# The last stage of a two-layer diffusion block: one token's eight expert rows added on VectorE and GpSimd, or on TensorE and VectorE

## The reference, cut to what matters

```python
def reference(...):
    ...
    for layer in range(2):
        ...                                   # attention, then the residual h_lat
        f_lat = modulate(rmsnorm(h_lat, g_ffn[layer]), sh_fl, sc_fl)
        if last:
            y = moe_ffn(f_lat, ...)           # per token: 8 routed experts, weighted, + a shared one
            h_lat = h_lat + gt_fl * y         # gate of the last layer
    return rmsnorm(h_lat, g_final)            # [1, 512, 1024], float32
```

## Time and profile before

| what | value |
|---|---|
| median of 3 runs (lowest to highest) | 2790.37 us (2789.46 to 2794.35) |
| the profiled execution's own time | 2796.55 us |
| its span, first to last instruction | 2794.8 us |
| last stage, first DMA issue to the end of the span | 2720.6 to 2794.8 us |
| busy between 2720 and 2795 | DVE 49.53, POOL 21.29, ACT 7.05, PE 0.00 us |

### The profile page before, as it was taken

The page is one execution under the profiler, slowest core; times in us unless marked ns, Lnnn a source line. Parts: engine busy times, 40 slices in busy tenths (PEclk is TensorE's granted clock), DMA queues, the critical chain, the costliest instruction groups (busy, mean ns, idle before and its releaser), DMA issues. The chain is left out here.

```text
span 2794.8 us, 34685 instructions
## 1 busy us (share of the span) xinstructions
PE 2368.1 (85%) x13774; PEld 1310.1 (47%) x13774; DVE 829.1 (30%) x1597; ACT 652.9 (23%) x1390; POOL 342.2 (12%) x282
## 2 busy tenths in 40 slices
PE   7899899897969999999991779996876988888860
PEld 3454577675534333333330678885743333333320
DVE  2232344533700000000003845555352000000007
ACT  1111333421112121121111344444210211111111
POOL 1000000021321111111110000000213111111103
PEclk9999999997989999999996889998988999999985
DMA  7465200012179999999965611100236999999956
GB/s 309 166 226 197 91 1 1 35 61 85 81 291 347 375 392 385 398 365 377 378 242 201 242 40 35 36 23 34 84 144 252 387 408 414 420 415 388 419 241 268
DMA packets 121023, 646.59 MB, mean 231 GB/s; under 512 B 19000, under 2 KB 30264, under 8 KB 60704
## 3 DMA queue, kind: packets, MB, share of 16 engines
q1 hardware_dynamic: 91456, 558.31, 50.9%
q0 software_dynamic: 28256, 83.95, 7.6%
q10 hardware_dynamic: 1152, 2.11, 0.2%
HBM read 604.38 MB, written 57.75 MB: 237 GB/s over the span
## 5 line engine op out<-in xcount | busy, mean ns | idle before, releaser
L1578 PE MATMUL F_psG<-gu_w,F_xT 128*32 128x512 f32 (+2 forms) x4448 | 708.4, 613 | 62.4 <-DMA gu_w<-in_we_up_dram 57.7
L1578 PEld LDWEIGHTS F_psG<-gu_w,F_xT 128*32 128x32 f32 (+2 forms) x4448 | 227.5, 123 | 471.9 <-issue 461.3
L1721 DVE TENSOR_TENSOR F_hh<-F_sil,F_psG 128x256 f32<-128x256 f32 x96 | 40.4, 421 | 1098.9 <-ACT F_sil L1665 1098.9
L1592 PE MATMUL F_psY<-d_w,F_hT 128*32 128x512 f32 (+2 forms) x2224 | 351.6, 599 | 3.0 <-ACT F_hT L1668 3.0
L1522 POOL DMA_INDIRECT y_d<-F_yb,sca x94 | 94.5, 1005 | 996.0 <-ACT F_yb L1671 996.0
L1665 ACT ACTIVATE F_sil<-F_psG 128x256 f32<-128x256 f32 x96 | 36.9, 384 | 671.9 <-PE F_psG L1578 671.9
L1592 PEld LDWEIGHTS F_psY<-d_w,F_hT 128*32 128x32 f32 (+2 forms) x2224 | 102.4, 120 | 180.6 <-issue 167.8
L1671 ACT ACTIVATE F_yb<-F_psY,wgt 128x1024 f32<-128x1024 f32 x96 | 107.0, 1115 | 291.7 <-PE F_psY L1592 291.7
L1571 PEld LDWEIGHTS F_psX<-cst,F_xb 128*128 128x128 f32 x768 | 95.7, 194 | 105.9 <-issue 71.4
L1571 PE MATMUL F_psX<-cst,F_xb 128*128 128x128 f32 x768 | 112.1, 290 | 32.0 <-DMA F_xb<-f_d,F_gi 27.2
L149 PE MATMUL I_psC<-I_w_hi,I_aT_hi 128*128 128x384 f32 (+1 forms) x336 | 112.6, 335 | 28.8 <-DVE I_aT_lo L2116 25.2
(11 more groups left out here) (342 smaller groups left out, 3166.0 us busy)
## 6 DMA issues: line engine op xcount, KB each, us to landing
gu_w<-in_we_gate_dram SPq DMA_DIRECT2D x130, 1024.0 KB, 6.6
gu_w<-in_we_up_dram SPq DMA_DIRECT2D x130, 1024.0 KB, 9.1
d_w<-in_we_down_dram SPq DMA_DIRECT2D x130, 1024.0 KB, 8.9
h<-in_w_ada_dram SPq DMA_DIRECT2D x40, 1024.0 KB
I_ring<-y_d SPq DMA_DIRECT2D x24, 1024.0 KB
H_y<-y_d SPq DMA_DIRECT2D x4, 4096.0 KB
I_w_raw<-in_wc_in_dram SPq DMA_DIRECT2D x32, 384.0 KB
wq<-in_w_ada_dram SPq DMA_DIRECT2D x8, 1024.0 KB, 4.6
```

The source lines that it names most:

```text
L1578: ins = nc.tensor.matmul(psG[c:c + n].rearrange("p (v f) -> p v f", v=2), xT[:, k, c:c + n], moe.gu[s][:, :, k], start=(k == 0), stop=(k = ...
L1592: ins = nc.tensor.matmul(psY[c:c + w, n], hT[:, j, k, c:c + w], moe.d[s][:, k, n * 512:(n + 1) * 512], start=(k == 0), stop=(k == KF - 1))
```

## The change

`stage_combine` is replaced by `stage_last`, which is written for this one call.

- SP loads each tile in 4 pieces of 2 rows (1 MB, 8 KB to a partition), 16 pieces in all. Each piece has a place of its own in SBUF (`rows`) and a semaphore of its own, so no load waits for anything.
- DVE takes pieces 0 and 1 of a tile: one addition of 2048 columns and one of 1024 (in place).
- PE takes pieces 2 and 3: it multiplies each of the 4 rows with the identity and accumulates them in PSUM (`psA`, two buffers of two banks). A bank holds 512 columns, so each row takes 2 products, and a tile takes 8.
- DVE then adds the PE's sum to its own, multiplies with the gate and adds to the residual, half by half: 6 instructions of 512 columns. POOL does nothing any more.
- ACT's work and the normalisation are as before. DVE waits once for both constants, ahead of its first addition.

```diff
-                            sp.dma_start(y8[:, t % 2], rows_of[t]).then_inc(s_ac[t % 2], 16)
+                        for t in range(NL):
+                            for n in range(PIECES):
+                                sp.dma_start(y[t][:, n], rows_of[t, :, 2 * n:2 * n + 2]).then_inc(s_y[PIECES * t + n], 16)
...
+                    @block.tensor
+                    def _(pe):
+                        for t in range(NL):
+                            if t >= 2:
+                                pe.wait_ge(s_acc, 2 * (t - 1))
+                            for n in range(PIECES - ON_PE, PIECES):
+                                pe.wait_ge(s_y[PIECES * t + n], 16)
+                                for b in range(2):
+                                    for k in range(2):
+                                        ins = nc.tensor.matmul(psA[:, t % 2, b], ident, y[t][:, n, k, b * 512:(b + 1) * 512],
+                                                               start=(n == PIECES - ON_PE and k == 0), stop=(n == PIECES - 1 and k == 1))
+                                    if n == PIECES - 1:
+                                        ins.then_inc(s_pe, 1)
...
-                            link(nc.vector.tensor_tensor(y[:, 0:4], y[:, 0:4], y[:, 4:8], ALU.add))
-                            link(nc.vector.tensor_tensor(y[:, 0:2], y[:, 0:2], y[:, 2:4], ALU.add))
-                            nc.vector.tensor_tensor(ac[:, t % 2], y[:, 0], y[:, 1], ALU.add).then_inc(s_sum, 1)
...
-                                nc.gpsimd.tensor_tensor(ac[:, t % 2], ac[:, t % 2], gate[:, 0 if t < NL else 1], ALU.mult).then_inc(s_g, 1)
-                                pool.wait_ge(s_g, t + 1)
-                                nc.gpsimd.tensor_tensor(h[:, t], h[:, t], ac[:, t % 2], ALU.add).then_inc(s_h, 1)
...
+                        dve.wait_ge(s_v, 32)
+                        for t in range(NL):
+                            for n in range(PIECES - ON_PE):
+                                dve.wait_ge(s_y[PIECES * t + n], 16)
+                            link(nc.vector.tensor_tensor(y[t][:, 0], y[t][:, 0], y[t][:, 1], ALU.add))
+                            link(nc.vector.tensor_tensor(y[t][:, 0, 0], y[t][:, 0, 0], y[t][:, 0, 1], ALU.add))
+                            if t >= 1:
                                 normed(t - 1)
+                            for b in range(2):
+                                c = slice(b * 512, (b + 1) * 512)
+                                dve.wait_ge(s_pe, 2 * t + b + 1)
+                                link(nc.vector.tensor_tensor(ac[:, t % 2, c], y[t][:, 0, 0, c], psA[:, t % 2, b], ALU.add))
+                                link(nc.vector.tensor_tensor(ac[:, t % 2, c], ac[:, t % 2, c], gate[:, c], ALU.mult))
+                                ins = nc.vector.tensor_tensor(h[:, t, c], h[:, t, c], ac[:, t % 2, c], ALU.add)
+                                ins.then_inc(s_acc, 1)
+                            dve.wait_ge(s_acc, 2 * t + 2)
+                            dve.sem_inc(s_h, 1)
+                        normed(NL - 1)
```

More of the change, by code:

```diff
@@ L1736, in _, with stage_last @@
                                 rows(s_xv)
-        def stage_combine(l, nt, aT):
+        def stage_last():
+            PIECES, ON_PE = TOPK // 2, 2
             with ExitStack() as ctx:
[L1743 to L1746, removed]
+                S = lambda n: sem(f"H_{n}_s")
+                T = lambda n, shape, dt=F32: sb(ctx, f"H_{n}", shape, dt)
+                rows = T("rows", [P, NL, PIECES, 2, D])
+                y = [rows[:, t] for t in range(NL)]
                 ac = T("ac", [P, 2, D])
-                gate = T("gate", [P, nv, D])
-                amul = T("amul", [P, nv, D])
-                aadd = T("aadd", [P, nv, D])
+                gate = T("gate", [P, D])
+                gain = T("gain", [P, D])
                 an = T("an", [P, 2, D])
[L1752 to L1759, removed]
+                st = T("st", [P, NL, 3])
+                junk = ps(ctx, "H_junk", [P, D])
+                psA = ps(ctx, "H_psA", [P, 2, 2, 512])
+                s_y = [S(f"y{g}") for g in range(PIECES * NL)]
+                s_v, s_pe, s_h, s_rt, s_out0, s_acc = S("v"), S("pe"), S("h"), S("rt"), S("o"), S("acc")
+                s_out, s_act, s_dve = [S("out0"), S("out1")], S("act"), S("dve")
+                rows_of = y_d[1].rearrange("(t p k) d -> t p k d", p=P, k=TOPK)
                 with nc.Block() as block:
@@ L1776, in _ @@
                         link = Chain(act, s_act)
[L1777 to L1793, removed]
+                        act.dma_start(gate[:], mod_rows(1, 0, 5)).then_inc(s_v, 16)
+                        act.dma_start(gain[:], a["g_final"].rearrange("(o d) -> o d", o=1).to_broadcast([P, D])).then_inc(s_v, 16)
+                        for t in range(NL):
+                            act.wait_ge(s_h, t + 1)
+                            link(nc.scalar.activation(junk[:], h[:, t], ACT.Square, accum_out=st[:, t, 0:1]))
+                            nc.scalar.activation(st[:, t, 1:2], st[:, t, 0:1], ACT.Sqrt, bias=eps, scale=1.0 / D).then_inc(s_rt, 1)
                     @block.vector
@@ L1813, in normed @@
                             if t >= 2:
[L1814 to L1823, removed]
@@ L1846, in _ @@
[L1846 to L1856 removed]
+                                dve.wait_ge(s_out[t % 2], 16 * (t // 2))
@@ L2368, in build @@
         moe_ctx.close()
-        stage_combine(1, NL, None)
+        stage_last()
         end_stage()
```

41 lines of the change are left out of this document (6 added, 35 removed).

## The result

The changed kernel takes 2777.18 us (median of 6 runs, 2774.83 to 2780.77) where the kernel before took 2793.96 in the same set of runs (2789.46 to 2796.61). The two medians differ by 16.8 us; the ratio estimated from the runs, 0.9946 with a 95% interval of 0.9935 to 0.9957, stands for some 15 us. Either way it is faster, by about half a per cent. A second set with the changed kernel and the kernel before gave 0.9954 (0.9941 to 0.9967).

The account below looks back on a forecast made before the run. The last stage was taken as bound by VectorE, stretched by GpSimd: 13.6 us a tile, falling to 9.50. Residuals end at 2772.5, plus 6.7 gives 2779.2, 15.6 earlier; 2790.4 - 15.6 = 2774.8 us, range 2770.5 to 2784.

Parts of the forecast that it names:

- the start of the loads: Last stage's loads: 1.02 MB until 2724.0, then 420 GB/s, so constants and pieces 0 and 1 landed at 2729.1.
- VectorE as the bound, and its price a tile: Last stage: VectorE's work sets the pace, 9.50 us a tile where it was 13.6.
- GpSimd as the reason for the long instructions: Last stage: GpSimd running beside VectorE added 2.1 us each to the 4096 addition and the result.
- GpSimd was not what stretched VectorE: Rival, last stage: the result stays at 3.39 us for three tiles, 6.3 us lost, 2781.1 us; chance 0.06.
- VectorE's wait for both constants costs nothing: Ahead of VectorE's first addition: constants land at the same time as the pieces it needs, so no time lost.
- The dip at tile 2: TensorE, after 3.0 us of idling ahead of tile 2: the products take 1.7 us longer.
- Slower transfers: Rival, last stage's loads: small pieces move at 360 GB/s, a gain of 11.1 us, 2779.3 us; chance 0.12.
- TensorE at the low level throughout: Rival, last stage: clock stays at 0.50, 14.06 us a tile, 2792.4 us; chance 0.09.
- The identity's load exposed at the low level: Rival, TensorE: 0.34 us identity loads stand between records, 1.22 us a record, median 2814.2 us; chance 0.04.
- The earlier clock: Rival, TensorE: clock rises early, VectorE's tile 0 wait is shorter, 1.2 us better, 2773.6 us; chance 0.07.

Follow-up runs that it names:

- e2: Kernel before with gate and residual moved from GpSimd to VectorE, loads of 4 MB kept: stage 65.8 us, median 2783.09 us, ratio 0.9972.
- e6: Changed kernel with one 4 MB load a tile, each with its own place, instead of pieces: stage 67.9 us, median 2786.10 us, ratio 0.9975.
- e4: Changed kernel plus two GpSimd instructions that nobody waits for after each of tiles 0 to 2: stage 72.9 us, median 2789.94 us.
- e7: Changed kernel with six of eight rows added on TensorE and two on VectorE: stage 63.8 us, median 2781.09 us, ratio 0.9957.
- e10: Changed kernel with 11 extra TensorE products at the stage's start, and gate and gain loaded before the last layer's routing: stage 56.4 us, median 2775.24 us.
- e11: Changed kernel plus one pair of unneeded GpSimd instructions during VectorE's wait for tile 0: stage 62.0 us, median 2779.78 us, ratio 0.9956.
- e12: The changed kernel run once more, unaltered: stage 62.5 us, median 2778.09 us, ratio 0.9954 to the kernel before.
- e5: Changed kernel plus 11 TensorE products on constants ahead of tile 0, to bring its clock up: stage 59.6 us, median 2778.49 us, ratio 0.9951.
- e8: Changed kernel without TensorE, all eight rows added on VectorE: stage 71.8 us, median 2789.08 us, ratio 0.9986.
- e3: Changed kernel with gate and residual back on GpSimd, half of the rows on TensorE: stage 72.5 us, median 2791.56 us, ratio 0.9997.
- e1: Kernel before with only its loads changed to 16 pieces with own places: stage 75.7 us, median 2794.06 us, ratio 1.0011.
- e9: Changed kernel with gate and residual on GpSimd and VectorE's result moved behind the next tile's halves: stage 66.9 us, median 2783.64 us, ratio 0.9972.

## Why the prediction was right, and where its sizes were off

The forecast of 2774.8 us is 2.4 below the median of 2777.2 and the range holds it. Part of that nearness is chance: the forecast started from a median of 2790.4 of three runs, where the kernel before had 2794.0 in the set of the result. The mechanism is better judged by the stage, 14.0 us shorter where 15.6 were forecast. Step by step, in stage time:

| step | forecast | measured |
|---|---|---|
| constants and pieces 0 and 1 landed, VectorE starts | +8.5 | +10.85 |
| piece 2 landed, TensorE starts | +11.0 | +13.05 |
| TensorE's tile 0 | 9.6 | 9.52 |
| VectorE's wait for it | 6.8 | 6.56 |
| tile 1 of TensorE | 7.03 | 7.13 |
| tile 2 of TensorE (a dip of 1.7 after the gap) | 8.7 | 7.11 |
| VectorE, a tile | 9.50 | 9.39 |
| end of the last residual to the end of the span | 6.7 | 6.93 |
| stage | 58.6 | 60.2 |

**The mis-sized term is the start of the loads**, "landed at 2729.1". I had taken the first 3.4 us from the kernel before, 1.02 MB; here they moved 201 x 3.4 = 0.68 MB. The next stretch went at 397 GB/s and not 420. And when VectorE was let go, 0.68 + 397 x 7.4 = 3.62 MB had come in all, not the 3.15 of the constants and two pieces: 0.47 MB of later pieces had gone ahead. At 420 GB/s these are 0.8, 0.4 and 1.1 us, together the 2.35 that are missing. It is the pieces that slow the start: in the first 3.4 us of the stage the three kernels with 4 MB loads (before, e2, and e6, which differs from the changed kernel in the loads alone) moved 299 to 318 GB/s, and all with pieces 193 to 224. Whether the packets' size or the number of transfers does it stays open. The rest of the forecast partly made up for the 2.35 us: from VectorE's start to the last residual it had 43.4 us, and 42.45 were measured.

**VectorE as the bound, and its price a tile**: right, to 0.11 us. **GpSimd as the reason for the long instructions**: right; e2 gives 4.2 us a tile back, e4 takes them again with work that nobody needs. With it the rival "GpSimd was not what stretched VectorE" falls. Of e2's 8.4 us, though, 3.2 are no hold-up of VectorE: they come from the gate and residual of the last tile, which took 5.7 us on GpSimd and take 2.5 on VectorE.

**"VectorE's wait for both constants costs nothing"**: true to about 0.4 us. In e7 TensorE starts on piece 1 at +10.43, and VectorE is let go by the constants at +10.87: they end nearly with the first pieces. But that hangs on the small packets (+25.1 in e6), and the constants' megabyte is not free: with it moved away, VectorE starts 3.3 us earlier (e10).

**The dip at tile 2** did not come in the profiled execution and did in others, at tile 2 (e11) or tile 3 (e12), and there it cost more than I took: 10.1 us a tile and not 8.7, with 1.29 and 1.99 us of waiting for VectorE. It is a spread of some 2 us from run to run.

**The other rivals.** Slower transfers: refuted, beyond the slow start, by 423 GB/s over 33 us. TensorE at the low level throughout: refuted by the 1.00 from 2745 to 2755. The identity's load exposed at the low level: refuted; at the granted clock of 0.50 in tile 0 the loads, 0.34 us each, follow one another every 0.85 us (2727.23, 2728.09, 2728.94) and not every 1.22, so they lie beside the products. The earlier clock: e5 made it happen, for 0.6 us of stage where I had 1.2 for it, as the pieces' arrival then sets the pace.

**What I did not foresee** is how the parts hang together. Of the 14.0 us, GpSimd's idleness alone gives 8.4 and the pieces alone -1.5; but the pieces give 7.7 in the changed kernel, by way of the constants' landing (e6), and TensorE's half, worth 11.6 without GpSimd (e8), is worth 3.2 as long as GpSimd does the rest (e3 against e1), or 8.8 without the loop of waits (e9). Moving the result of tile 2 into the wait for the last root, as e2 has it, was not tried in the changed kernel.

## What to carry to other kernels

Before giving GpSimd the small change of a VectorE-bound loop, look in the timeline for the same VectorE instruction with and without GpSimd beside it: here two GpSimd instructions cost VectorE 4.2 us a tile and would have cost it 2.5 had it done them itself. Load small constants that an engine waits for well before the large transfers, or keep the packets beside them small: their queue gets one packet for one (48 to 48 before), and the pieces' 7.7 us came that way. Compare stage times and not only medians when the part ahead of a change varies by more than the change is worth.

## What the runs showed that I had not expected

- **VectorE and GpSimd take turns, a whole instruction at a time**, in both directions: beside VectorE, GpSimd's 2.34 us became 4.27, and VectorE's 1.23 became 3.24 (e4).
- **TensorE's clock after a short pause is not settled by the pause.** Of 14 pauses of 2.8 to 2.9 us ahead of a tile (in the changed kernel, e3, e4, e5, e9 to e12), nine were followed by tiles of 7.1 us and five by slower ones (8.49 in e3, 10.08 in e11, 10.13 in e12; in e4 and e9 tiles 2 and 3 ran on without a gap, in 17.06 and 17.04 us for both). What decides it stays open.
- **A constant's landing depends on the other queue's packets**: the same two loads landed at +25.1 us beside packets of 32 KB and at +10.9 beside 8 KB.
